# MLA attention: values of two heads at a time in the two column halves, and queries in two halves of 272 columns

## The reference

```
kv = (ckv_all @ w_ukv).reshape(B, keys, 16, 64 + 64)          # keys and values of 16 heads
s  = einsum('bqhd,bkhd->bhqk', qn, k_nope) + einsum('bqhd,bkd->bhqk', qr, k_rope)
p  = softmax(where((q_pos // 64)[:, None] >= (k_pos // 64)[None, :], s * scale, -inf))
o  = einsum('bhqk,bkhd->bqhd', p, v)                          # 64 values a head
out = o.reshape(B, L, 16 * 64) @ w_out
```

## Time and profile before

| | us |
|---|---|
| median of 3 runs | 2523.39 (2520.73 to 2523.8) |
| the profiled execution | 2520.12 |
| its span, first to last instruction | 2518.2 |
| attention of the MLA layer in it | about 1539 to 1746 |

### The profile page before, as it was taken

The page is one execution under the profiler, slowest core; times in us unless marked ns, Lnnn a source line. Parts: engine busy times, 40 slices in busy tenths (PEclk is TensorE's granted clock), DMA queues, the critical chain, the costliest instruction groups (busy, mean ns, idle before and its releaser), DMA issues. The chain is left out here.

```text
span 2518.2 us, 32513 instructions
## 1 busy us (share of the span) xinstructions
PE 2066.4 (82%) x12936; PEld 1700.9 (68%) x12936; DVE 1600.8 (64%) x1729; ACT 1301.5 (52%) x1514; POOL 261.8 (10%) x329
## 2 busy tenths in 40 slices
PE   2689777886574999999998188998759999999990
PEld 1679774886574888888887054555747888888870
DVE  0345107454646888888886513665368888888883
ACT  1233612222323777777775342443237777777763
POOL 0123120330000010101110010000000010101000
PEclk6789888997786999999999598999969999999995
DMA  9167450000343899999997512002338999999974
GB/s 335 51 247 284 171 195 10 3 5 1 132 143 127 321 367 372 374 380 380 366 364 263 200 69 105 1 1 79 121 116 318 372 367 365 366 366 370 369 272 169
DMA packets 160041, 561.47 MB, mean 223 GB/s; under 512 B 33757, under 2 KB 39930, under 8 KB 126738
## 3 DMA queue, kind: packets, MB, share of 16 engines
q1 hardware_dynamic: 137938, 539.04, 57.9%
q0 software_dynamic: 21952, 20.32, 2.4%
HBM read 557.84 MB, written 50.70 MB: 242 GB/s over the span
## 5 line engine op out<-in xcount | busy, mean ns | idle before, releaser
L1954 DVE TENSOR_TENSOR ex_wl<-ring,ex_wh 128x2048 fp32r<-128x2048 f32 x384 | 867.9, 2289 | 112.5 <-ACT ex_wh L1909 112.5
L1909 ACT CAST ex_wh<-ring 128x2048 fp32r<-128x2048 f32 x384 | 712.4, 1910 | 0.0
L238 PE MATMUL ex_p<-ex_wh,ex_xh 128*128 128x512 f32 x1024 | 414.3, 405 | 8.3 <-DVE ex_xl L1959 8.3
L238 PE MATMUL ex_p<-ex_wl,ex_xh 128*128 128x512 f32 x1024 | 402.3, 393 | 0.0
L238 PE MATMUL ex_p<-ex_wh,ex_xl 128*128 128x512 f32 x1024 | 401.7, 392 | 0.0
L238 PEld LDWEIGHTS ex_p<-ex_wh,ex_xh 128*128 128x128 f32 x1024 | 194.5, 190 | 46.1 <-DVE ex_xl L1959 9.9
L238 PEld LDWEIGHTS ex_p<-ex_wl,ex_xh 128*128 128x128 f32 x1024 | 194.0, 189 | 42.7
L238 PEld LDWEIGHTS ex_p<-ex_wh,ex_xl 128*128 128x128 f32 x1024 | 194.5, 190 | 36.7
L238 PE MATMUL ex_py<-ex_wh,ex_gh 128*128 128x512 f32 x512 | 200.2, 391 | 2.8 <-DVE ex_gl L1975 2.8
L238 PE MATMUL ex_py<-ex_wl,ex_gh 128*128 128x512 f32 x512 | 200.2, 391 | 0.0
L238 PE MATMUL ex_py<-ex_wh,ex_gl 128*128 128x512 f32 x512 | 199.9, 390 | 0.0
(11 more groups left out here) (414 smaller groups left out, 3811.3 us busy)
## 6 DMA issues: line engine op xcount, KB each, us to landing
ring<-in_moe_w SPq DMA_DIRECT2D x384, 1024.0 KB, 7.3
ring<-in_ada_w SPq DMA_DIRECT2D x24, 2048.0 KB, 12.2
ring<-in_ab_w_in SPq DMA_DIRECT2D x7, 2048.0 KB, 9.7
mod<-mod SPq DMA_DIRECT2D x16, 512.0 KB, 7.1
cb_y<-yrow SPq DMA_DIRECT2D x16, 512.0 KB, 9.6
xres<-x SPq DMA_DIRECT2D x12, 512.0 KB, 2.7
x<-xres SPq DMA_DIRECT2D x12, 512.0 KB, 9.4
ring<-in_ab_w_out SPq DMA_DIRECT2D x2, 2048.0 KB, 11.9
```

Source lines behind the costliest of these rows:

```text
L238: ins = nc.tensor.matmul(out, a, b, start=first and n + m == 0, stop=last and n == len(terms) - 1 and m == 2)
L1909: nc.scalar.copy(part(wh, u), g.view(base + u)).then_inc(hi_ready, 1)
L1954: nc.vector.tensor_tensor(part(wl, u), g.view(base + u), part(wh, u).bitcast(F32), ALU.subtract).then_inc(lo_ready, 1)
```

## The change

Three things. The values are multiplied for two heads at once, at t = 1 of every second head and once at the end: for each tile of keys first the even head into the lower half of `po`, then the odd head into the upper half, that is in turn in the two column halves of the array. The turned probabilities of a head get 13 tiles of 128 columns in which the tile of queries t and keys j is number t + 3j; so what one step turns lies at one stride (one copy by ScalarE), and what one tile of keys needs lies together (one product). The sample's two pieces lie in the two tiles left free, 7 and 10. There are three such buffers instead of two. And the queries are multiplied in two halves of 272 columns instead of 512 and 32, so that `pre` holds them as two banks, and what reads them has views with a split.

```diff
-        pT = sb("pT", [P, 2, sum(SEQ - P * j for j in range(NT - 1))])
-        pTs = sb("pTs", [P, 2, 2, DSEQ])
+        pT = sb("pT", [P, 3, 13, P])
...
+        halves = [slice(0, TOK // 2), slice(TOK // 2, TOK)]
+        split = lambda ap: ap.rearrange("p (a n) -> p a n", a=2)
...
-        row = lambda j: sum(SEQ - P * i for i in range(j))
+
+        turned_to = lambda b, t: pT[:, b, t:4 * t + 1:3, :]
+        turned_row = lambda b, j: pT[:, b, 4 * j:3 * j + 4, :]
+        own = lambda b, i, rows: pT[0:rows, b, 7 + 3 * i, 0:DSEQ]
...
                     for k in range(QR // P):
-                        nc.tensor.matmul(pre[:, 0, :], m.wq[:, k, h, :], m.cqT[:, k, 0:SEQ], start=k == 0, stop=k == QR // P - 1)
-                        last = nc.tensor.matmul(pre[:, 1, 0:DSEQ], m.wq[:, k, h, :], m.cqT[:, k, SEQ:TOK], start=k == 0, stop=k == QR // P - 1)
+                        for a, at in enumerate(halves):
+                            last = nc.tensor.matmul(pre[:, a, 0:TOK // 2], m.wq[:, k, h, :], m.cqT[:, k, at], start=k == 0, stop=k == QR // P - 1)
...
-                def values(h):
-                    c, at, b = h * MV, slice(MV * (h % 2), MV * (h % 2) + MV), h % 2
-                    pe.wait_ge(pT_ready, NT * (h + 1))
-                    if h % 2 == 0 and h:
-                        pe.wait_ge(oh_ready, h // 2)
-                        pe.wait_ge(ol_ready, h // 2)
+                def values(pair):
+                    heads = [(h * MV, slice(MV * (h % 2), MV * (h % 2) + MV), h % 3) for h in (2 * pair, 2 * pair + 1)]
+                    pe.wait_ge(pT_ready, NT * (2 * pair + 2))
+                    if pair:
+                        pe.wait_ge(oh_ready, pair)
+                        pe.wait_ge(ol_ready, pair)
                     for j in range(NT - 1):
-                        nc.tensor.matmul(po[at, 0, j * P:SEQ], m.v[:, j, c:c + MV], pT[:, b, row(j):row(j + 1)],
-                                         start=j == 0, stop=j == NT - 2)
-                    nc.tensor.matmul(po[at, 1, 0:DSEQ], m.v[:, NT - 1, c:c + MV], pTs[:, b, 0, :], start=True, stop=False)
-                    nc.tensor.matmul(po[at, 1, 0:DSEQ], m.v[0:DSEQ, NT, c:c + MV], pTs[0:DSEQ, b, 1, :],
-                                     start=False, stop=True).then_inc(o_done, 1)
+                        for c, at, b in heads:
+                            nc.tensor.matmul(po[at, 0, j * P:SEQ], m.v[:, j, c:c + MV], turned_row(b, j), start=j == 0, stop=j == NT - 2)
+                    for c, at, b in heads:
+                        nc.tensor.matmul(po[at, 1, 0:DSEQ], m.v[:, NT - 1, c:c + MV], own(b, 0, P), start=True, stop=False)
+                    for c, at, b in heads:
+                        last = nc.tensor.matmul(po[at, 1, 0:DSEQ], m.v[0:DSEQ, NT, c:c + MV], own(b, 1, DSEQ), start=False, stop=True)
+                    last.then_inc(o_done, 1)
...
-                    if t == 1 and h:
-                        values(h - 1)
-                values(MH - 1)
+                    if t == 1 and h and h % 2 == 0:
+                        values(h // 2 - 1)
+                values(HALF - 1)
...
-                    if t == 0 and h >= 2:
-                        act.wait_ge(o_done, h - 1)
+                    if t == 0 and h >= 3:
+                        act.wait_ge(o_done, (h - 1) // 2)
                     if t < NT - 1:
-                        for j in range(t + 1):
-                            at = row(j) + (t - j) * P
-                            last = nc.scalar.copy(pT[:, h % 2, at:at + P], pt[:, i % 2, j, :])
+                        nc.scalar.copy(turned_to(h % 3, t), pt[:, i % 2, 0:t + 1, :]).then_inc(pT_ready, 1)
```

More of the change, by code:

```diff
@@ L2486, in keep_queries @@
                     act.wait_ge(q_done, h + 1)
-                    nc.scalar.activation(qT[0:NOPE, h % 2, :], flat[0:NOPE, 0:TOK], ACT.Copy, scale=QW ** -0.5).then_inc(q_nope, 1)
+                    nc.scalar.activation(split(qT[0:NOPE, h % 2, :]), pre[0:NOPE, :, 0:TOK // 2], ACT.Copy, scale=QW ** -0.5).then_inc(q_nope, 1)
                 def turned_round(i):
@@ L2491, in turned_round @@
                     act.wait_ge(t_done, i + 1)
-                    if t == 0 and h >= 2:
-                        act.wait_ge(o_done, h - 1)
+                    if t == 0 and h >= 3:
+                        act.wait_ge(o_done, (h - 1) // 2)
                     if t < NT - 1:
-                        for j in range(t + 1):
-                            at = row(j) + (t - j) * P
-                            last = nc.scalar.copy(pT[:, h % 2, at:at + P], pt[:, i % 2, j, :])
-                    else:
-                        nc.scalar.copy(pTs[:, h % 2, 0, :], pt[:, i % 2, 0, 0:DSEQ])
-                        last = nc.scalar.copy(pTs[0:DSEQ, h % 2, 1, :], pt[0:DSEQ, i % 2, 1, 0:DSEQ])
-                    last.then_inc(pT_ready, 1)
+                        nc.scalar.copy(turned_to(h % 3, t), pt[:, i % 2, 0:t + 1, :]).then_inc(pT_ready, 1)
+                    else:
+                        nc.scalar.copy(own(h % 3, 0, P), pt[:, i % 2, 0, 0:DSEQ])
+                        nc.scalar.copy(own(h % 3, 1, DSEQ), pt[0:DSEQ, i % 2, 1, 0:DSEQ]).then_inc(pT_ready, 1)
                 def out_hi(pair):
-                    act.wait_ge(o_done, 2 * pair + 2)
+                    act.wait_ge(o_done, pair + 1)
                     nc.scalar.copy(oh[:, pair, :], po_flat[:, 0:TOK]).then_inc(oh_ready, 1)
@@ L2538, in turn_queries @@
                     dve.wait_ge(q_done, h + 1)
-                    nc.vector.tensor_tensor(turned[64:96, :], flat[64:96, 0:TOK], rope[64:96, :], ALU.mult)
-                    ch(nc.vector.tensor_tensor(qT[64:96, h % 2, :], flat[96:128, 0:TOK], rope[96:128, :], ALU.mult))
+                    nc.vector.tensor_tensor(split(turned[64:96, :]), pre[64:96, :, 0:TOK // 2], split(rope[64:96, :]), ALU.mult)
+                    ch(nc.vector.tensor_tensor(split(qT[64:96, h % 2, :]), pre[96:128, :, 0:TOK // 2], split(rope[96:128, :]), ALU.mult))
                     nc.vector.tensor_tensor(qT[64:96, h % 2, :], turned[64:96, :], qT[64:96, h % 2, :], ALU.add).then_inc(q_rope, 1)
```

## The result

The changed kernel takes 2524.87 us (median of 20 runs, 2521.16 to 2532.6), the kernel before 2520.86 (20 runs): a ratio of 1.0018, 95% interval 1.001 to 1.0026. It is 4.0 us slower, where a gain of 0.8 was forecast. The profiled execution of the changed kernel has a span of 2524.0 us, 5.8 more than before. The two part in the attention.

A forecast was written before the change was run, and what follows sets the result against it. In attention, VectorE's chain before step 2's turning, which TensorE's values only fill, and the queries were taken to set the beat. Gains of 11.0 us less losses of 10.2 gave 0.8 off 2523.4: 2522.5 us, range 2512 to 2529.

The forecast's parts named there:

- The hole: TensorE's wait for VectorE before turning step 2; bare in odd heads once values go, about 2.3 us idle.
- The queries: Each head's query products as twelve instructions of 272 columns: 0.41 us less a head, 6.6 us over 16 heads.
- The odd heads: Heads 1 to 13 lose their values; VectorE's wait for step 4's scores goes: 0.35 us each, 2.5 in all.
- The even heads: Heads 2 to 14 run two heads' values side by side in the old place: 0.05 us lost each, 0.4 in all.
- the strict program order: Skill's rule that matmuls start and end in order; by it the paired values would make the sum 2.7 us worse.
- The end: Head 15 loses its values, which delayed step 4's scores; the rest up to the final pair comes 1.9 us earlier.
- the final pair: Last two heads' values at the attention's end: one head's time, plus 1.0 us lost to a possible half clock.
- The new wait of ScalarE and the copies: ScalarE's wait on a pair's values before a head's first copy, and four copies merged into one: no time counted.
- the price of a fall: Clock dropping to half after an odd head's hole: 1.46 us each, read from head 0; six falls, 8.8 us.
- the likely case: Clock falls in most odd heads at head 0's price: 2522.5 us, chance 0.66.
- the clock stays down twice as long: Rival for odd heads' thin steps 2 to 4: 2.9 us a fall, six falls 17.5, total 2531.3; chance 0.11.
- the prediction's signs of being wrong: Odd heads' idle much shorter than 2.3 us, clock staying at 1.00 through them, or the pair taking near 5 us.

The follow-up runs named there:

- e6: The kernel of e1 with a pair's prompt values multiplied one head after the other instead of in turn; 2529.63 us, ratio 1.0026.
- e1: Changed kernel with two unread 480-column products in odd heads 1 to 13, between step 4's scores and step 2's turning; 2506.93 us, ratio 0.993.
- e11: The changed kernel run once more without any edit; 2527.32 us, ratio 1.0009 to the kernel before.
- e3: Changed kernel with the queries as before (512 and 32 columns), so the paired values alone; 2544.75 us, ratio 1.0079 to the kernel before.
- e7: Changed kernel with each pair's values split by key tiles: first tile and sample in the even head, other tiles in the odd; 2522.4 us, ratio 0.9992.
- e8: Changed kernel, hole left bare, with one unread 480-column product in each of steps 3 and 4 of odd heads 1 to 13; 2532.67 us, ratio 1.0024.
- e10: A second, identical run of the kernel of e1; 2510.93 us, ratio 0.9944 to the kernel before.
- e4: The kernel of e1 with one unread 480-column product per odd head instead of two; 2515.41 us, ratio 0.9972 to the kernel before.
- e5: The kernel of e1 with four unread 480-column products per odd head instead of two; 2514.89 us, ratio 0.9969 to the kernel before.
- e9: Changed kernel, the odd head's values except its first key tile moved to the odd hole, one unread product in head 1; 2509.35 us, ratio 0.9952.
- e2: The kernel before with only the queries changed, to two halves of 272 columns; 2515.29 us, ratio 0.9971.

## Why the prediction was wrong

*Right by its own steps.* The hole: 2.35 us of idle time, ended by VectorE, as read from head 0. The queries: 0.44 us a head, forecast 0.41; that forecast rounded a half to 0.23 us before multiplying by twelve, and unrounded (2.81 + 0.10) it would have been 0.36, so its closeness is in part luck. The odd heads: 10.74 - 9.98 = 0.76 without a fall, less 0.44 for the queries leaves 0.32, forecast 0.35; that VectorE's chain and not the values' 2.61 us sets the beat was the reading that mattered most, and it held. The even heads: 2.62 us to the scores of step 4, forecast 2.66 and 2.61 before; the halves run together. By the strict program order that the Trainium skill states (TensorE: Matmul & The Clock Gate, Part 3: Packing small matmuls) the sum was to be 2.7 us worse. The sixteen instructions in 2.20 us, and the start of line 2457 ahead of earlier ones in e6, speak against that order in this case. The end came 2.1 us earlier, forecast 1.9, and the final pair had no fall, where I had counted 1.0. The new wait of ScalarE and the copies don't show in the beats, as forecast: one 128x512 copy took 0.573 us (forecast 0.59, before 0.77 for the four), and the beats of e1 leave no room for a stall.

*The step that failed* is the price of a fall in the part on the clock. I forecast six at 1.46 us, 8.8 in all; there were five at 2.6 to 4.2, 17.0 in all. With the forecast price the same five would have been 7.3 and the stage 12.8 - 7.3 = 5.5 us shorter than before, not 4.2 longer. So the term alone carries the miss, and turns the sign. The 1.46 was read from one fall, head 0's in the kernel before, during which the clock was down from 1559.8 to 1563.0, 3.4 us; the five lasted 6.8 and 10.2 us. It isn't the price of head 0 either: behind the same hole the clock fell for 6.8 us in e11 and in e3, at 3.3 and 3.1 us of price. Of the three falls of head 0 on record the forecast had met the cheap one.

Why the falls of the odd heads last longer is shown in part. Behind an odd head's hole come an even one's scores and turnings, thin work with TensorE waiting on VectorE, and the next dense work are the queries, 6.3 us after the hole (1700.37 to 1706.65). Of eighteen falls in bare odd holes with nothing put behind them (five in the changed kernel's first execution, five in e11, seven in e3, one in e7) seventeen lasted 6.8 or 10.2 us, and one, head 1's in e3, 3.4. e8 puts products 0.6 to 1.1 us behind the hole, and all three falls are 3.4 us long, with 1.5 to 1.7 us of price; e1 fills the hole itself and they vanish, in 42 odd holes of six executions (e1, e10, e4, e5, e6, e9). But dense work further behind didn't keep falls short. Behind head 0's hole stands the projection of the next keys, in the kernel before 3.7 us after it (1557.80):

```profile
1561.52 1.80 PE L2408 MATMUL ma_pre<-mla_ckvT,mla_wk 128*128 128x512 f32 x2
```

There the fall was 3.4 us long. In e3's head 0 the keys stand 3.8 us behind the hole (1554.18 to 1557.96), in e11's 4.4 and in e7's head 12 4.0, and in all three the half clock lasted 6.8 us. Why the one was short and these were long no run here shows.

The forecast had this as a rival, "the clock stays down twice as long", with the right place, the thin steps of an odd head, and 2.9 us a fall; it had a chance of 0.11. Its own rows held both lengths, head 0's and the longer stretch that stood at 1546.1 and still at 1550.22, and only the shorter one became the price of the likely case. What the rival gave, 2531.3, is 6.4 too high: 2.5 from its base, 2523.4, where the twenty runs give 2520.9; 2.2 from the gains, 12.8 where it had 10.6; 1.0 from the final pair; and 0.5 from the falls, 17.5 against 17.0.

None of the prediction's signs of being wrong came: the hole is 2.35 us, the clock falls, the pair takes 2.6. They didn't ask how long a fall lasts. And that 2524.87 lies only 2.4 us from the forecast 2522.5 is luck: the forecast stands on a median of three runs, and with the same gain of 0.8 on the median of twenty it would have been 2520.1, 4.8 us away on the other side of no change.

*A part that the sum didn't have.* Head 0's own fall, 3.4 us in the kernel before, came in neither the changed kernel's first profile nor in e2's. The halves are not what prevents it: with them it came in e11, without them in e3. Its hole is bare in all thirteen executions on record, and it fell in three.

*What else stays open.* Why the entry to the experts, whose code no run here changed, has its stretch at full clock in some executions and not in others, and with it why e7, with a stage 5 us shorter, is no faster as a whole. No experiment was aimed at it. Nor why heads 3 and 7 are spared in both executions of the changed kernel, and why head 1 fell for 10.2 us in the one and 6.8 in the other.

## What to carry to other kernels

Work that hides under another engine's chain costs nothing while it is there, but its removal is not free: the idle stretch that it leaves can cost more by the clock than all else that the change wins. Before work is taken out of such a hole, price a fall from several of them in several executions, and not from one: in one place, head 0, it cost 1.5, 3.1 and 3.3 us. Bare odd holes cost up to 4.2; only work put close behind the hole (e8) kept all falls at 1.5 to 1.7. Where the work must go, leave most of the hole filled (e9; the thinner filling of e7 fell once) or change only what is on the path (e2).

## What the runs showed of the hardware

- The half clock came in stretches of about 3.4, 6.8 and 10.2 us in this stage, and the price of a fall went with the length: 1.4 to 1.7 us for 3.4 (kernel before, e3, e8), 2.6 to 3.3 for 6.8 (changed kernel, e11, e3, e7), 4.1 to 4.2 for 10.2 (changed kernel, e11, e7).
- A bare hole of 2.3 to 2.4 us was followed by a fall in all seven odd heads of e3, in the same five of seven in both executions of the changed kernel, in three of seven in e8, and in three of thirteen executions in head 0.
- One unread product of 480 columns in the hole (the rest still bare) went with a clock of 1.00 through all odd heads of one execution, and four cost no more than 0.46 us a beat. Needed work that left 1.02 us idle was followed by a fall once in e7.
- Two column halves fed in turn ran sixteen instructions in the 2.20 us that eight take for one; head after head they took 3.76, and a later instruction for the one half started ahead of earlier ones for the other.
- After the attention the clock stood at 0.50 for 13 and 44 us, with 10 us at 1.00 between, in the kernel before, and for 75 us at one go in six other executions, with the same code there; the part behind the attention took 771.8 us in the first and 776.9 to 781.6 in those.
